# Prompt attention with its query tiles taken in turns from both ends, two banks for the transposed probabilities, and a bank for each output tile

## The chip, the cores and the metric

The kernel runs on one core of one Trainium2 chip. The metric is the device time of one execution in microseconds (us). The engines are named as in the profile: PE is TensorE (PEld its weight loads), DVE is VectorE, ACT is ScalarE, POOL is GpSimd, SP is SyncE, which here issues most DMAs. PSUM, the memory that PE writes its results to, has eight banks of 2 KB in each of its 128 partitions.

## The reference

One decoder layer for a prompt of 1024 tokens and for eight samples of four tokens. The change lies in the prompt's attention. Its core is this: for every head, the query at position i meets the keys at or before it, gets a bias by distance, and a softmax:

```
logits = einsum(q, k) * ATT_SCALE + bias          # bias by T5 bucket of i - j
probs  = softmax(where(mask, logits, -1e30))
out    = einsum(probs, v)
o_b    = gates[0] * o_cmp + gates[1] * o_slc + gates[2] * o_win
```

Three kinds of it are computed in the stage: mixer A (eight heads; the three dilated windows are merged into one table of biases and masks), the selected branch of mixer B and its window branch of 512 tokens (eight query heads each, in two groups that share keys and values). The gates are sigmoids of projected values. All query tiles are independent of each other, so they may be computed in any order.

## The kernel before

`prompt_attention` handles three kinds times four pairs of heads, twelve iterations (`it`), of eight units each (`u`, 96 in all). A unit is one tile of 128 queries (`qt`, 0 to 7) for the two heads of a pair. It meets `nk` key tiles of 128 keys: `qt + 1` of them, and in the last kind at most five. `parts(u)` gives these numbers. In this kernel `qt` is `u % 8`, so within an iteration the units grow from one key tile to eight (36 tiles in all, 30 in an iteration of the last kind), and then the next iteration starts with one again.

The order of work is written out by hand, engine by engine, in steps `s`. In step `s`

- PE computes the scores of unit s into `psS` (two chunks of 512 keys are held, L672), then the transposes of the probabilities of unit s-2 into banks of `psT` (four 128x128 blocks to a bank, L690), then the products with the values of unit s-3 into `psO` (L711) and, in the same tile of `psO`, a transpose of the softmax weights (L717);
- DVE adds the bias and takes the maximum of unit s (`logits`, L821, then L827 and L831, which writes the negated maximum `nm`), copies those banks of unit s-2 from `psT` to `PT` that are its own (`copies`, L847), takes a reciprocal for unit s-1 (L835) and multiplies out unit s-3 (`finish`, L859);
- ACT copies the other banks of unit s-2 (L789), then computes the exponentials of unit s (L795) and copies the weight row `Rs` of unit s-3 (L802);
- POOL widens the reciprocals (L753, L758), adds up the branches in `mixT` (L769), and reverses the queries of the next iteration (L738).

The banks of transposed probabilities are numbered through the stage. DVE copies every bank whose number leaves 2 when divided by 3 (`on_dve`), ACT the others. `psT` has three banks, so PE may write bank b once bank b-3 was copied. Both tiles of `psO` lie in one bank, and the value products of unit u wait until `finish` of unit u-1 is done (semaphore `s_wt`). With `psS` at four banks, all eight banks are in use.

The gates are brought into reversed order by one product (L705) into `psO` ahead of the values of unit 8; ACT turns them into sigmoids (L776) at the start of step 11, and PE waits for that. SP loads queries, keys, biases and values of iteration it+1 once all units of iteration it-1 are finished (`load`).

Of the kernel before, what the change touches and what calls it, by code (L numbers as in the profile page):

```python
# [9 lines left out]
ACT = mybir.ActivationFunctionType  # L10
AXX = mybir.AxisListType.X

P = 128
# [520 lines left out]

def prompt_attention(nc, io, scr, mixT, wo, cv, s_mix, s_wo, s_cvl):
    QT = SEQ // P
    NKIND = 3
    NIT = NKIND * 4
    U = NIT * QT

    kinds = [
        dict(tab="tabA", tab0=7172 - A0, q0=0, k0=0, v="new_a_v_p", gate=None, back=QT),
        dict(tab="tabS", tab0=7172, q0=8, k0=8, v="new_slc_v_p", gate=1, back=QT),
        dict(tab="tabW", tab0=7172 - W0, q0=8, k0=10, v="vw", gate=2, back=LW // P),
    ]

    def parts(u):

        it, qt = u // QT, u % QT
        j0 = max(0, qt - kinds[it // 4]["back"])  # L550
        return it, it // 4, it % 4, qt, j0, qt + 1 - j0

    chunk0, bank0 = [0], [0]
    for u in range(U):
        nk = parts(u)[5]
        chunk0.append(chunk0[-1] + -(-nk // 4))
        bank0.append(bank0[-1] + -(-2 * nk // 4))

    def on_dve(bank):
        return bank % 3 == 2  # L560

    def copied(bank):

        return bank - bank // 3, bank // 3

    with ExitStack() as stack:
        m = Mem(nc, stack, "pa")
        gates = m.sb("gates", [P, QT, 24])
        gsig = m.sb("gsig", [P, QT, 24])
        ident = m.sb("ident", [P, P])  # L570
        flip = m.sb("flip", [P, P])
# [6 lines left out]
        PT = m.sb("PT", [P, 3, 2 * SEQ])  # L578
# [6 lines left out]
        tmp = m.sb("tmp", [P, 4, P])  # L585
        Rs = m.sb("Rs", [P, 4, P])
        psS = m.ps("psS", [P, 2, 2, 512])
        psT = m.ps("psT", [P, 3, 512])
        psO = m.ps("psO", [P, 2, 2 * P])
        s_id = m.sem("identity_loaded")  # L590
        s_gl = m.sem("gates_loaded")
        s_mc = m.sem("compressed_rows_loaded")
        s_gf = m.sem("gates_flipped")
        s_gs = m.sem("gates_ready")
# [8 lines left out]
        s_ca = m.sem("probs_t_copied_by_act")  # L603
        s_cd = m.sem("probs_t_copied_by_dve")
# [4 lines left out]
        s_wt = m.sem("weighted")  # L609
# [50 lines left out]
        @block.tensor  # L660
        def _(pe):
            def scores(u):
                it, ki, p, qt, j0, nk = parts(u)
                i = it % 2
                for c in range(chunk0[u], chunk0[u + 1]):
                    k0 = (c - chunk0[u]) * 512
                    w = min(512, nk * P - k0)
                    if c >= 2:
                        pe.wait_ge(s_lg, 2 * (c - 1))
                    for h in range(2):  # L670
                        r = slice(h * HD, h * HD + HD)
                        pe.matmul(psS[:, c % 2, h, 0:w], qT[r, i, qt * P:qt * P + P],  # L672
                                  kT[r, i, j0 * P + k0:j0 * P + k0 + w], start=True, stop=True).then_inc(s_qk, 1)

            def transposes(u):
                nk = parts(u)[5]
                if u == 0:
                    pe.wait_ge(s_id, 16)
                pe.wait_ge(s_ex, 2 * (u + 1))
                for b in range(bank0[u], bank0[u + 1]):  # L680
                    if b >= 3:
                        na, nd = copied(b - 2)
                        if on_dve(b - 3):
                            pe.wait_ge(s_cd, nd)
                        else:
                            pe.wait_ge(s_ca, na)
                    x0 = 4 * (b - bank0[u])
                    for x in range(x0, min(x0 + 4, 2 * nk)):
                        j, h = x // 2, x % 2
                        mm = pe.transpose(psT[:, b % 3, (x - x0) * P:(x - x0) * P + P],  # L690
                                          L[:, u % 3, h, j * P:j * P + P], ident[:, :])
                    mm.then_inc(s_tr, 1)

            def values(u):
                it, ki, p, qt, j0, nk = parts(u)
                i = it % 2
                na, nd = copied(bank0[u + 1])
                pe.wait_ge(s_ca, na)
                if nd:
                    pe.wait_ge(s_cd, nd)  # L700
                if u:
                    pe.wait_ge(s_wt, u)
                if u == QT:
                    pe.wait_ge(s_gl, 32)
                    pe.matmul(psO[:, u % 2, 0:QT * 24], flip[:, :],  # L705
                              gates[:, :, :].rearrange("p t n -> p (t n)"), start=True, stop=True).then_inc(s_gf, 1)
                    pe.wait_ge(s_gs, 1)
                for j in range(nk):
                    for h in range(2):
                        v0 = h * HD if ki == 0 else 0  # L710
                        mm = pe.matmul(psO[h * HD:h * HD + HD, u % 2, 0:P], V[:, i, j0 + j, v0:v0 + HD],  # L711
                                       PT[:, u % 3, (2 * j + h) * P:(2 * j + h) * P + P],
                                       start=(j == 0), stop=(j == nk - 1))
                        if j == nk - 1:
                            mm.then_inc(s_pv, 1)
                pe.wait_ge(s_rg, u + 1)
                pe.transpose(psO[:, u % 2, P:2 * P], rgB[:, u % 4, :, :].rearrange("p h d -> p (h d)"),  # L717
                             ident[:, :]).then_inc(s_pv, 1)

            for s in range(U + 3):  # L720
                if s < U:
                    if s % QT == 0:
                        it = s // QT
                        pe.wait_ge(s_ld[it % 2], 96 * (it // 2 + 1))
                        pe.wait_ge(s_qr, it + 1)
                    scores(s)
                if 2 <= s < U + 2:
                    transposes(s - 2)
                if s >= 3:
                    values(s - 3)  # L730
# [40 lines left out]
        @block.scalar  # L771
        def _(act):
            for s in range(U + 3):
                if s == QT + 3:
                    act.wait_ge(s_gf, 1)
                    nc.scalar.activation(gsig[:, :, :], psO[:, QT % 2, 0:QT * 24].rearrange("p (t n) -> p t n", t=QT),  # L776
                                         ACT.Sigmoid).then_inc(s_gs, 1)
                if 2 <= s < U + 2:
                    u = s - 2
                    nk = parts(u)[5]  # L780
                    if u >= 3:
                        act.wait_ge(s_pv, 3 * (u - 2))
                    for b in range(bank0[u], bank0[u + 1]):
                        if on_dve(b):
                            continue
                        x0 = 4 * (b - bank0[u]) * P
                        w = min(512, 2 * nk * P - x0)
                        act.wait_ge(s_tr, b + 1)
                        nc.scalar.activation(PT[:, u % 3, x0:x0 + w], psT[:, b % 3, 0:w], ACT.Copy).then_inc(s_ca, 1)  # L789
                if s < U:  # L790
                    w = parts(s)[5] * P
                    act.wait_ge(s_nm, s + 1)
                    for h in range(2):
                        x = L[:, s % 3, h, 0:w]
                        nc.scalar.activation(x, x, ACT.Exp, bias=nm[:, s, h:h + 1], scale=1.0,  # L795
                                             accum_out=sm[:, s, h:h + 1]).then_inc(s_ex, 1)
                if s >= 3:
                    u = s - 3
                    act.wait_ge(s_pv, 3 * (u + 1))
                    if u >= 4:  # L800
                        act.wait_ge(s_wt, u - 3)
                    nc.scalar.activation(Rs[:, u % 4, :], psO[:, u % 2, P:2 * P], ACT.Copy).then_inc(s_rs, 1)  # L802

        @block.vector
        def _(dve):
# [31 lines left out]
            def copies(u):  # L837
                nk = parts(u)[5]
                for b in range(bank0[u], bank0[u + 1]):
                    if not on_dve(b):  # L840
                        continue
                    x0 = 4 * (b - bank0[u]) * P
                    w = min(512, 2 * nk * P - x0)
                    if u >= 3:
                        dve.wait_ge(s_pv, 3 * (u - 2))
                    dve.wait_ge(s_tr, b + 1)
                    dve.tensor_copy(PT[:, u % 3, x0:x0 + w], psT[:, b % 3, 0:w]).then_inc(s_cd, 1)  # L847

            def finish(u):
                it, ki, p, qt, j0, nk = parts(u)  # L850
# [2318 lines left out]
```

## Time and profile before

| | |
|---|---|
| median of 3 runs | 2502.0 us (2500.79 to 2505.6) |
| profiled execution | 2500.79 us |
| its span in the trace | 2499.0 us |
| prompt attention in the trace | about 1068 to 1482 us |
| PE, DVE, ACT, POOL busy, share of the whole span | 91%, 39%, 23%, 19% |
| PE, DVE, ACT busy, 1068 to 1482 us | 354, 237, 241 us of 414 |

The shares are averages over stages with different limits. In the stage that is changed, PE shows busy for 85% of the time, but with matmuls that overlap and whose ends are modelled, and with gaps at semaphores in every step; DVE and ACT are each busy for somewhat less than 60%. What sets its length is to be read from the waits and from the order of events in single steps.

### The profile page before, as it was taken

The numbers are of one execution on the slowest core, as the hardware profiler recorded it, in microseconds if no ns is written. First come the engines' busy times: TensorE is split into PE (matmuls) and PEld (weight loads), VectorE is DVE, ScalarE is ACT, GpSimd is POOL, SyncE is SP. The second block draws the span as 40 slices with busy tenths as digits, with TensorE's granted clock in tenths as the row PEclk, the third lists the DMA queues.
The fourth block names the chain that finished last, engine by engine and source line by source line (L and its number), as shares of the span: only waits on it lengthen the run. The fifth ranks groups of instructions, "written<-read, shape, count | busy, mean of one in ns | idle before, by whom it ended". The sixth has DMA issues, their size and how long they took to land. (4 is left out here: it accounts for less than half of the span.)

```text
span 2499.0 us, 34990 instructions
## 1 busy us (share of the span) xinstructions
PE 2268.6 (91%) x13904; PEld 1475.1 (59%) x13904; DVE 977.2 (39%) x2333; ACT 572.6 (23%) x1255; POOL 466.1 (19%) x664
## 2 busy tenths in 40 slices
PE   7999997999488687678888889999999999999998
PEld 3445666666254555445555654488888888744443
DVE  3001002333133354355555642277677675500210
ACT  3000002333022133255555641111101111100110
POOL 1314211221100344200121220022233222100000
PEclk8999997999788899899999999999999999999999
DMA  6712114776476777641222422165656542500110
GB/s 230 230 69 79 46 41 183 284 285 242 154 262 246 273 297 308 248 140 61 60 77 77 128 66 78 59 219 185 224 182 236 190 149 68 205 32 0 61 37 17
DMA packets 162360, 376.33 MB, mean 151 GB/s; under 512 B 44231, under 2 KB 100911, under 8 KB 144272
## 3 DMA queue, kind: packets, MB, share of 16 engines
q1 hardware_dynamic: 128284, 148.68, 18.9%
q0 software_dynamic: 25216, 149.43, 15.6%
q10 hardware_dynamic: 8698, 75.99, 8.8%
q8 instruction: 111, 1.82, 0.3%
q14 instruction: 51, 0.41, 0.1%
HBM read 345.71 MB, written 99.65 MB: 178 GB/s over the span
## 5 line engine op out<-in xcount | busy, mean ns | idle before, releaser
L2674 PE MATMUL ff_ps<-ff_hx,ff_aw 128*128 128x264 f32 x2464 | 550.1, 386 | 0.9 <-DVE ff_hx L2913 0.9
L2674 PEld LDWEIGHTS ff_ps<-ff_hx,ff_aw 128*128 128x128 f32 x2464 | 467.3, 190 | 80.8 <-issue 1.2
L369 PE MATMUL in_ps<-in_w,in_xT 128*128 128x512 f32 (+1 forms) x512 | 199.6, 545 | 0.0
L795 ACT ACTIVATE pa_L<-pa_L,pa_nm 128x640 f32<-128x640 f32 (+3 forms) x192 | 142.0, 741 | 143.7 <-DVE pa_nm L831 143.5
L369 PEld LDWEIGHTS in_ps<-in_w,in_xT 128*128 128x128 f32 x512 | 95.2, 190 | 93.6 <-issue 84.9
L821 DVE CUSTOM_DVE_ANT_0 pa_L<-pa_psS,pa_T 128x512 f32<-128x512 f32 (+3 forms) x288 | 138.4, 530 | 29.1 <-PE pa_psS L672 28.1
L491 DVE TENSOR_SCALAR in_yout<-in_ps 128x512 f32<-128x512 f32 (+2 forms) x44 | 26.1, 593 | 300.3 <-PE in_ps L369 190.9
L711 PE MATMUL pa_psO<-pa_PT,pa_V 128*64 128x128 f32 x1632 | 112.6, 282 | 33.6 <-DVE pa_tmp L859 21.9
L690 PE MATMUL pa_psT<-pa_ident,pa_L 128*128 128x128 f32 x816 | 115.1, 281 | 22.2 <-DVE pa_PT L847 14.1
L672 PE MATMUL pa_psS<-pa_kT,pa_qT 64*128 64x512 f32 (+3 forms) x576 | 115.3, 506 | 21.2 <-POOL pa_qT L738 18.4
L1064 DVE COPY cmp_KT<-cmp_psT 128x512 f32<-128x512 f32 x128 | 88.6, 692 | 97.6 <-PE cmp_psT L980 96.8
L690 PEld LDWEIGHTS pa_psT<-pa_ident,pa_L 128*128 128x128 f32 x816 | 87.2, 141 | 64.7 <-issue 29.5
L711 PEld LDWEIGHTS pa_psO<-pa_PT,pa_V 128*64 128x64 f32 x1632 | 90.7, 139 | 52.2 <-issue 47.9
L383 PE MATMUL in_ps<-in_xT,in_w 128*128 128x352 f32 x384 | 113.9, 459 | 0.0
L990 PE MATMUL cmp_psH<-cmp_KT,pre_w 64*64 64x512 f32 x1024 | 113.3, 592 | 0.0
L2633 PE MATMUL ff_ps<-ffn_G 128*128 128x512 f32 x256 | 111.9, 596 | 0.0
L2856 ACT ACTIVATE ff_work<-ff_work 128x1056 f32<-128x1056 f32 x22 | 23.8, 1083 | 369.8 <-DVE ff_work L3008 369.8
L3035 DVE TENSOR_TENSOR ff_work<-ff_ps,ff_work 128x512 f32<-128x512 f32 (+1 forms) x18 | 12.3, 685 | 238.0 <-PE ff_ps L2752 139.3
L1077 ACT ACTIVATE cmp_KT<-cmp_psT 128x512 f32<-128x512 f32 x128 | 76.5, 598 | 104.4 <-PE cmp_psT L980 104.3
L2099 PE MATMUL sb_psT<-sb_ident,sel_space 128*128 128x128 f32 x512 | 72.2, 290 | 28.8 <-ACT sel_space L2245 15.0
L2702 PE MATMUL ff_ps<-ff_hx,ffn_G 128*128 128x512 f32 x224 | 97.4, 592 | 0.0
L383 PEld LDWEIGHTS in_ps<-in_xT,in_w 128*128 128x128 f32 x384 | 72.8, 190 | 40.5 <-issue 0.2
(381 smaller groups left out, 3042.2 us busy)
## 6 DMA issues: line engine op xcount, KB each, us to landing
out_new_a_k_s<-in_cache_a_k ACTq DMA_DIRECT2D x8, 4088.0 KB
out_new_a_v_s<-in_cache_a_v ACTq DMA_DIRECT2D x8, 4088.0 KB
ff_aw<-in_w_up SPq DMA_DIRECT2D x44, 512.0 KB, 7.1
in_w<-in_w_in SPq DMA_DIRECT2D x5, 2048.0 KB, 19.0
sel_space<-in_cache_a_k SPq DMA_DIRECT2D x8, 1024.0 KB
sel_space<-in_cache_a_v SPq DMA_DIRECT2D x8, 1024.0 KB
ff_hx<-in_w_down SPq DMA_DIRECT2D x14, 512.0 KB, 4.3
sel_space<-in_cache_a_k SPq DMA_DIRECT2D x24, 256.0 KB
```

The costliest lines, as they stand in the source:

```text
L369: mm = pe.matmul(ps[0:n, b, 0:width], xT[:, k, t * P:t * P + n], w[:, ch % WBUF, k, 0:width], start=(k == 0), stop=(k == KC - 1))
L383: mm = pe.matmul(ps[:, b, 0:n], w[:, ch % WBUF, k, c * P:c * P + P], xT[:, k, r0:r0 + n], start=(k == 0), stop=(k == KC - 1))
L672: pe.matmul(psS[:, c % 2, h, 0:w], qT[r, i, qt * P:qt * P + P], kT[r, i, j0 * P + k0:j0 * P + k0 + w], start=True, stop=True).then_inc(s_q ...
L690: mm = pe.transpose(psT[:, b % 3, (x - x0) * P:(x - x0) * P + P], L[:, u % 3, h, j * P:j * P + P], ident[:, :])
L711: mm = pe.matmul(psO[h * HD:h * HD + HD, u % 2, 0:P], V[:, i, j0 + j, v0:v0 + HD], PT[:, u % 3, (2 * j + h) * P:(2 * j + h) * P + P], star ...
L795: nc.scalar.activation(x, x, ACT.Exp, bias=nm[:, s, h:h + 1], scale=1.0, accum_out=sm[:, s, h:h + 1]).then_inc(s_ex, 1)
L821: dve.tensor_tensor_reduce(L[:, u % 3, h, 512 * x:512 * x + n], psS[:, c % 2, h, 0:n], T[:, it % 2, h, SEQ - w + 512 * x:SEQ - w + 512 * x ...
L990: mm = pe.matmul(psH[odd_t * HD:odd_t * HD + HD, p % 2, h, 0:w], pre.w1[r, kv, t + odd_t, :], x(r, odd_t), start=first, stop=last, tile_po ...
L1064: copy(KT[:, n % 2, 4 * x:4 * x + 4, j * P:j * P + P], psT[:, u % 3, :].rearrange("p (t n) -> p t n", t=4)).then_inc((s_ca, s_cd)[which], 1)
L2633: mm = pe.matmul(ps[:, j % 6, :], mixT[:, k, t * P:t * P + P], wo[:, k, half * 512:half * 512 + 512], start=(k == 0), stop=(k == KC - 1))
L2674: mm = pe.matmul(ps[:, bank_of(x, j, g), 0:H2], aw[:, j % 2, at, k, :], hx[:, bt, k, g * H2:g * H2 + H2], start=(k == 0), stop=(k == KH - 1))
L2702: mm = pe.matmul(ps[:, bank[i] + half, :], G[:, k, t * P:t * P + P], wd(k)[:, half * 512:half * 512 + 512], start=(k == 0), stop=(k == NFF ...
```

## The change

Four edits, all in `prompt_attention`:

1. `parts(u)` takes its query tile from `TURNS = [0, 7, 1, 6, 2, 5, 3, 4]`. The units of an iteration then have 1, 8, 2, 7, 3, 6, 4, 5 key tiles (in the last kind 1, 5, 2, 5, 3, 5, 4, 5).
2. `psT` has two banks instead of three: PE may write bank b once bank b-2 was copied. Which banks DVE copies goes on by the same rule (number modulo 3).
3. `psO` is two whole banks, one for each tile; the values of unit u wait for `finish` of unit u-2.
4. The sigmoid of the gates is moved from the start of step 11 on ACT to its end, just ahead of the weight row of unit 8; the product that feeds it goes to the upper half of the bank, and PE waits for it only before the values of unit 10.

```
+    TURNS = [0, 7, 1, 6, 2, 5, 3, 4]
...
-        it, qt = u // QT, u % QT
+        it, qt = u // QT, TURNS[u % QT]
...
-        psT = m.ps("psT", [P, 3, 512])
-        psO = m.ps("psO", [P, 2, 2 * P])
+        psT = m.ps("psT", [P, 2, 512])
+        psO = m.ps("psO", [P, 2, 512])
...
-                    if b >= 3:
-                        na, nd = copied(b - 2)
-                        if on_dve(b - 3):
+                    if b >= 2:
+                        na, nd = copied(b - 1)
+                        if on_dve(b - 2):
                             pe.wait_ge(s_cd, nd)
                         else:
                             pe.wait_ge(s_ca, na)
...
-                if u:
-                    pe.wait_ge(s_wt, u)
+                if u >= 2:
+                    pe.wait_ge(s_wt, u - 1)
                 if u == QT:
                     pe.wait_ge(s_gl, 32)
-                    pe.matmul(psO[:, u % 2, 0:QT * 24], flip[:, :],
+                    pe.matmul(psO[:, u % 2, 2 * P:2 * P + QT * 24], flip[:, :],
                               gates[:, :, :].rearrange("p t n -> p (t n)"), start=True, stop=True).then_inc(s_gf, 1)
+                if u == QT + 2:
                     pe.wait_ge(s_gs, 1)
...
-                if s == QT + 3:
-                    act.wait_ge(s_gf, 1)
-                    nc.scalar.activation(gsig[:, :, :], psO[:, QT % 2, 0:QT * 24].rearrange("p (t n) -> p t n", t=QT),
-                                         ACT.Sigmoid).then_inc(s_gs, 1)
...
                     if u >= 4:
                         act.wait_ge(s_wt, u - 3)
+                    if u == QT:
+                        act.wait_ge(s_gf, 1)
+                        nc.scalar.activation(gsig[:, :, :], psO[:, u % 2, 2 * P:2 * P + QT * 24].rearrange("p (t n) -> p t n", t=QT),
+                                             ACT.Sigmoid).then_inc(s_gs, 1)
```

How the order moves (`pa_psS` is psS of this stage, and so on; sizes are those of one result): on PE, the first iteration, from the scores of unit 3 on. Before (scores of four key tiles, transposes of two, values of one; then five, three, two):

```order
L672 MATMUL pa_psS<-pa_kT,pa_qT 128x512 x2
L690 MATMUL pa_psT<-pa_ident,pa_L 128x128 x4
L711 MATMUL pa_psO<-pa_PT,pa_V 64x128 x2
L717 MATMUL pa_psO<-pa_ident,pa_rgB 128x128
L672 MATMUL pa_psS<-pa_kT,pa_qT 128x512 x2
L672 MATMUL pa_psS<-pa_kT,pa_qT 128x128 x2
L690 MATMUL pa_psT<-pa_ident,pa_L 128x128 x6
L711 MATMUL pa_psO<-pa_PT,pa_V 64x128 x4
L717 MATMUL pa_psO<-pa_ident,pa_rgB 128x128
```

And now, on PE at the same place (scores of seven key tiles, transposes of eight, values of one; then three, two, eight):

```order
L673 MATMUL pa_psS<-pa_kT,pa_qT 128x512 x2
L673 MATMUL pa_psS<-pa_kT,pa_qT 128x384 x2
L691 MATMUL pa_psT<-pa_ident,pa_L 128x128 x16
L713 MATMUL pa_psO<-pa_PT,pa_V 64x128 x2
L719 MATMUL pa_psO<-pa_ident,pa_rgB 128x128
L673 MATMUL pa_psS<-pa_kT,pa_qT 128x384 x2
L691 MATMUL pa_psT<-pa_ident,pa_L 128x128 x4
L713 MATMUL pa_psO<-pa_PT,pa_V 64x128 x16
L719 MATMUL pa_psO<-pa_ident,pa_rgB 128x128
```

Large scores now stand beside large transposes and small values, and small scores beside small transposes and large values. The sixteen transposes fill four banks of a `psT` that holds two.

On ACT, the same iteration, before, steps 4 to 6 (exponentials of five, six and seven key tiles):

```order
L789 ACTIVATE pa_PT<-pa_psT 128x256
L795 ACTIVATE pa_L,pa_sm<-pa_L,pa_nm 128x640 x2
L802 ACTIVATE pa_Rs<-pa_psO 128x128
L789 ACTIVATE pa_PT<-pa_psT 128x512
L795 ACTIVATE pa_L,pa_sm<-pa_L,pa_nm 128x768 x2
L802 ACTIVATE pa_Rs<-pa_psO 128x128
L789 ACTIVATE pa_PT<-pa_psT 128x512 x2
L795 ACTIVATE pa_L,pa_sm<-pa_L,pa_nm 128x896 x2
```

And now on ACT, steps 3 to 5 (exponentials of seven, three and six key tiles):

```order
L787 ACTIVATE pa_PT<-pa_psT 128x512 x3
L793 ACTIVATE pa_L,pa_sm<-pa_L,pa_nm 128x896 x2
L804 ACTIVATE pa_Rs<-pa_psO 128x128
L793 ACTIVATE pa_L,pa_sm<-pa_L,pa_nm 128x384 x2
L804 ACTIVATE pa_Rs<-pa_psO 128x128
L787 ACTIVATE pa_PT<-pa_psT 128x512 x2
L787 ACTIVATE pa_PT<-pa_psT 128x256
L793 ACTIVATE pa_L,pa_sm<-pa_L,pa_nm 128x768 x2
```

All of ACT's copies of a unit still stand ahead of the exponentials of the same step. On DVE the order within a step is the same as before; this is step 3 now, logits of seven key tiles, then the one bank of the unit of eight that is DVE's:

```order
L823 ISA pa_L,pa_mx<-pa_psS,pa_T 128x384
L823 ISA pa_mx 128x1
L829 TENSOR_TENSOR pa_mm<-pa_mx 128x2
L833 TENSOR_SCALAR pa_nm<-pa_mm 128x2
L849 COPY pa_PT<-pa_psT 128x512
L837 RECIPROCAL pa_rg<-pa_sm 128x2
L861 TENSOR_TENSOR ffn_G<-pa_psO,pa_Rs 128x128
```

DVE's copy comes behind the logits of a unit of seven key tiles, where before it came behind those of a unit two tiles larger than the one copied.

## Rows read from the trace of the kernel before

**Rows 1.** Waits, 1068 to 1482 us: engine, releaser; total us, times, longest us.
```profile
ACT pa_L L795 <- DVE pa_nm L831: 143.5, 76, 23.0
...
DVE pa_tmp L859 <- ACT pa_Rs L802: 99.0, 64, 3.0
...
PE pa_psO L711 <- DVE pa_tmp L859: 21.9, 35, 0.9
```

**Rows 2.** Timeline, a six-tile step: start, length, engine, line, instruction [idle before].
```profile
1262.92 0.29 DVE L859 TENSOR_TENSOR pa_tmp<-pa_psO,pa_Rs 128x128 f32<-128x128 f32 x1 [1.90 <-ACT pa_Rs L802]
1263.13 0.68 DVE L821 CUSTOM_DVE_ANT_0 pa_L<-pa_psS,pa_T 128x512 f32<-128x512 f32 x1
...
1265.35 0.17 DVE L831 TENSOR_SCALAR pa_nm<-pa_mm 128x2 f32<-128x2 f32 x1
1265.42 0.69 DVE L847 COPY pa_PT<-pa_psT 128x512 f32<-128x512 f32 x1
1265.55 0.94 ACT L795 ACTIVATE pa_L<-pa_L,pa_nm 128x768 f32<-128x768 f32 x1 [2.08 <-DVE pa_nm L831]
...
1267.69 0.29 DVE L859 TENSOR_TENSOR pa_tmp<-pa_psO,pa_Rs 128x128 f32<-128x128 f32 x1 [1.50 <-ACT pa_Rs L802]
```

**Rows 3.** Timeline, other starts of the finishing instruction L859.
```profile
1258.63 0.29 DVE L859 TENSOR_TENSOR pa_tmp<-pa_psO,pa_Rs 128x128 f32<-128x128 f32 x1 [1.14 <-ACT pa_Rs L802]
...
1272.94 0.29 DVE L859 TENSOR_TENSOR pa_tmp<-pa_psO,pa_Rs 128x128 f32<-128x128 f32 x1 [1.72 <-ACT pa_Rs L802]
...
1278.67 0.29 DVE L859 TENSOR_TENSOR pa_tmp<-pa_psO,pa_Rs 128x128 f32<-128x128 f32 x1 [1.93 <-ACT pa_Rs L802]
...
1281.69 0.29 DVE L859 TENSOR_TENSOR pa_tmp<-pa_psO,pa_Rs 128x128 f32<-128x128 f32 x1 [1.43 <-ACT pa_Rs L802]
...
1423.46 0.29 DVE L859 TENSOR_TENSOR pa_tmp<-pa_psO,pa_Rs 128x128 f32<-128x128 f32 x1 [1.47 <-ACT pa_Rs L802]
...
1426.98 0.29 DVE L859 TENSOR_TENSOR pa_tmp<-pa_psO,pa_Rs 128x128 f32<-128x128 f32 x1 [1.14 <-ACT pa_Rs L802]
```

**Rows 4.** Timeline, the first L859 and that of unit 92.
```profile
1077.03 0.29 DVE L859 TENSOR_TENSOR ffn_G<-pa_psO,pa_Rs 128x128 f32<-128x128 f32 x1 [1.68 <-ACT pa_Rs L802]
...
1474.28 0.29 DVE L859 TENSOR_TENSOR pa_tmp<-pa_psO,pa_Rs 128x128 f32<-128x128 f32 x1 [1.29 <-ACT pa_Rs L802]
```

**Rows 5.** Timeline, copies, transposes and value products where large follows small.
```profile
1275.98 0.69 DVE L847 COPY pa_PT<-pa_psT 128x512 f32<-128x512 f32 x1
...
1276.73 1.09 PE L690 MATMUL pa_psT<-pa_ident,pa_L 128*128 128x128 f32 x8 [0.77 <-DVE pa_PT L847]
...
1278.55 1.49 ACT L789 ACTIVATE pa_PT<-pa_psT 128x512 f32<-128x512 f32 x3
...
1279.55 1.53 PE L711 MATMUL pa_psO<-pa_PT,pa_V 128*64 128x128 f32 x24
...
1281.90 1.53 PE L690 MATMUL pa_psT<-pa_ident,pa_L 128*128 128x128 f32 x12
...
1283.09 1.08 ACT L789 ACTIVATE pa_PT<-pa_psT 128x512 f32<-128x512 f32 x2 [1.44 <-PE pa_psT L690]
```

**Rows 6.** Timeline, ScalarE around the sigmoid.
```profile
1108.15 1.28 ACT L776 ACT_TABLE_LOAD   x1
...
1109.68 0.33 ACT L776 ACTIVATE pa_gsig<-pa_psO 128x192 f32<-128x192 f32 x1 [0.25 <-PE pa_psO L705]
```

**Rows 7.** Stretches: length; busy PE, PEld, DVE, ACT, POOL; PEclk, DMA share, GB/s.
```profile
1070.00:1072.00 2.00, 2.00 (x7) 0.68 (x6) 1.43 (x10) 1.43 (x7) 0.29 (x1) 0.50 1.04 375
...
1241.00:1243.00 2.00, 0.59 (x6) 0.43 (x8) 1.37 (x8) 1.66 (x6) 0.00 (x0) 1.00 0.00 0
1243.00:1247.00 4.00, 4.00 (x32) 2.93 (x29) 0.79 (x4) 0.28 (x1) 0.81 (x2) 0.57 0.02 4
...
1265.00:1267.00 2.00, 2.00 (x15) 1.20 (x12) 1.12 (x6) 1.45 (x3) 0.73 (x2) 1.00 0.03 5
```

**Rows 8.** Timeline, the first load of a later iteration on SyncE's queue.
```profile
1254.82 0.32 SPq L623 DMA_DIRECT2D pa_qL<-scr_qT  x1
```

More of the change, by code:

```diff
@@ L689, in transposes @@
                         j, h = x // 2, x % 2
-                        mm = pe.transpose(psT[:, b % 3, (x - x0) * P:(x - x0) * P + P],
+                        mm = pe.transpose(psT[:, b % 2, (x - x0) * P:(x - x0) * P + P],
                                           L[:, u % 3, h, j * P:j * P + P], ident[:, :])
@@ L788, in _ @@
                         act.wait_ge(s_tr, b + 1)
-                        nc.scalar.activation(PT[:, u % 3, x0:x0 + w], psT[:, b % 3, 0:w], ACT.Copy).then_inc(s_ca, 1)
+                        nc.scalar.activation(PT[:, u % 3, x0:x0 + w], psT[:, b % 2, 0:w], ACT.Copy).then_inc(s_ca, 1)
                 if s < U:
@@ L846, in copies @@
                     dve.wait_ge(s_tr, b + 1)
-                    dve.tensor_copy(PT[:, u % 3, x0:x0 + w], psT[:, b % 3, 0:w]).then_inc(s_cd, 1)
+                    dve.tensor_copy(PT[:, u % 3, x0:x0 + w], psT[:, b % 2, 0:w]).then_inc(s_cd, 1)
             def finish(u):
```

## The prediction

> **What bounds the kernel now.** I read the waits of the attention stage first, then the timeline of single steps. The two longest waits of working engines point at each other: ACT waits for DVE's negated maximum before the exponentials (143.5 us over 76 times), and DVE waits for ACT's weight row before it finishes a unit (99.0 us in the two kinds of mixer B alone) [rows 1]. The wait that the change takes away, value products behind the finish of the unit before, shows 21.9 us in the same two kinds.
>
> The timeline of a step of six key tiles shows why the first two are a loop [rows 2]: finish at 1262.92, logits from 1263.13, maximum at 1265.35, exponentials from 1265.55, and the next finish at 1267.69, as soon as ACT has copied the weight row behind them. No PE instruction is in it. Finish to exponentials is 2.63 us (DVE's half), exponentials to finish 2.14 us (ACT's half), together 4.77. The order in which DVE and ACT do this doesn't change: the exponentials of step s stand between the logits of s and the finish at the end of s.
>
> The length of this loop follows from the number of key tiles of unit s. Five tiles take 1262.92 - 1258.63 = 4.29 us, eight 1278.67 - 1272.94 = 5.73 [rows 2, 3]: 0.48 per tile. Four tiles, with one chunk less, take 1426.98 - 1423.46 = 3.52, so that I take 3.04, 2.56 and 2.08 for three, two and one. That is 31.24 us for an iteration of 1 to 8 and 28.36 for one of the last kind. All twelve: 8 x 31.24 + 4 x 28.36 = 363.4 us.
>
> What the stage takes beyond it is the only thing that a better order can give back. From the first finish (end of step 3) to that of unit 92 (end of step 95) it is 1474.28 - 1077.03 = 397.25 us [rows 4]. The loop accounts for 363.4 less 11.2 of steps 0 to 3, so 352.2. 45.0 us are left, nearly all in the three or four steps after the turn from large to small. There the loop is short and PE has the largest transposes and value products to do: the step of one tile takes 1281.69 - 1278.67 = 3.02 us in place of 2.08 [rows 3], since the value products begin only at 1279.55 [rows 5].
>
> **The change, part by part.** *The turns.* Each step keeps its loop length, so 363.4 stays. PE's work is levelled. Transposes cost 0.22 us a tile (1.53 us for twelve, which is six tiles, 1.09 for eight), and value products the same (1.53 for six tiles) [rows 5], and scores about the same by their number of columns. With 0.56 for the gaps between the parts, as I read them at those starts, an iteration costs PE about 36 x 3 x 0.22 + 8 x 0.56 = 28.3 us against 31.24 of the loop. Following the starts through one iteration, PE is ready in every step but one: in the step of the large unit after the smallest, its scores come 0.05 to 0.4 us late in the first two kinds, and 0.7 in the last, where that step's loop is short. I take 8 x 0.3 + 3 x 0.7 = 4.5 us. So all of the 45.0 goes and 4.5 comes back. If PE keeps up everywhere this is 0; if PE set the time of the four small steps, as 3.02 against 2.08 did, it is 48 x 0.94 = 45.
>
> *A bank of its own for each output tile.* The wait of 21.9 us goes. Only where PE was late did it reach the loop, and that is in the 45.0 already. Nothing is added.
>
> *Two banks for the transposes.* This takes something away that the trace of before can't show. Within a step ACT's copies of unit s-2 stand ahead of its exponentials, and DVE's copy of unit s-2 stands behind its logits (the copy starts at 1265.42, after the maximum at 1265.35 [rows 2]). With three banks, bank b waits for bank b-3, and if DVE copies b-3 it copies b too: ACT never waits for a bank behind DVE's copy of the same unit. With two, the bank two behind one of DVE's is ACT's, and it can't be transposed before DVE is through with the logits. ACT then holds the exponentials behind this chain: logits, DVE copy, transposes, ACT copy. From the moment at which the exponentials could have started the price is: copy starts 0.13 earlier [rows 2], takes 0.69, PE starts 0.06 after its end (1276.73 against 1275.98 + 0.69), four transposes 0.66 (eight take 1.09, at 0.11 apiece), about 0.1 to ACT (at 1283.09 it starts behind eight transposes that began at 1281.90), and 0.5 until ACT goes on after a copy (three take 1.49, of which each occupies about 0.45 to 0.6) [rows 5]. The sum is 1.87. Where the late bank holds two blocks it is 0.22 less for PE and 0.2 less for the shorter copy: 1.45.
>
> It happens in units of three or four banks in which DVE has the first bank, or the second of four. Counting banks modulo 3 (20 in an iteration, 18 in the last kind), two of the large units of each iteration have it: in the first two kinds 11 times with a full bank and 5 times with a half one, in the last kind 8 times with a half one. So 11 x 1.87 + 13 x 1.45 = 39.4 us. All these lie in steps with large logits, and the loop has no slack there. Bounds: if ACT's other copies or late scores had delayed the step anyway, down to 24 x 0.8 = 19; if each also held up PE's values of the next step, 24 x 2.3 = 55. I take 39.4, since each piece has a row.
>
> *The sigmoid.* Before, a table load of 1.28 us, the sigmoid (0.33) [rows 6] and a second such load ahead of the exponentials stood in step 11, with DVE's logits beside them; what they cost is in the 45.0. Now the first load and the sigmoid come behind the exponentials of step 11, on the path: 1.6. The second comes ahead of step 12's exponentials, beside short logits: 0.4. I take 2.0, between 1.2 and 3.
>
> *The start.* PE begins at the lower clock (0.50 from 1070 to 1072 [rows 7]), and now with scores of eight tiles instead of two: 0.8.
>
> *Loads.* An iteration's loads start in the third step of the one before (1254.82 [rows 8]) and are through by about 1265 [rows 7]. POOL wants them in its seventh step, about 15 us behind the start now against 18 before. Covered by some 4 us.
>
> *The clock.* In a held-up step PE does nothing from its second bank to the end of the logits, up to 3.1 us. Between 1243 and 1247 the granted clock was 0.57 of full, of its levels of 2.4 and 1.2 GHz mostly the lower, and in the two microseconds before it fell PE was busy for 0.59 [rows 7]. At the lower one, value products in the next step come up to 1.7 late against a slack of 1.2. I take 0.5 us in 9 of the 24 steps, 4.5; 0 and 24 x 0.94 = 22.6 are the ends.
>
> *Sum.* 4.5 + 39.4 + 2.0 + 0.8 + 4.5 = 51.2 come and 45.0 go: 6.2 us more. On the profiled execution (2500.8, which is also the fastest of the three) that is 2507; on the median of 2502.0 it is 2508.
>
> **The rivals.**
>
> *The clock decides (slower by more).* Each held-up step is followed by a stretch at half clock. Then four transposes inside the chain take 0.44 more and the next step 0.5. 22.6 in place of 4.5 gives 24 us more, 2526. For it: idle stretches of up to 3.1 us now come twice an iteration, longer than the 1.4 us in the row before the fall. Against it: PE stood still at each turn of iteration before, and the stage's clock shows only this fall and one like it. The Trainium skill ("TensorE: Matmul & The Clock Gate", "Why this matters for your kernels") says in its table that idle gaps between bursts of matmuls put the engine back to its lower clock; by that rule most held-up steps would lose it, and this rival would hold.
>
> *The levelling wins (faster).* The hand-over costs less than the sum of its pieces, because in steps with large logits the first scores are late or DVE's maximum comes before the copies that ACT has to do anyway; it decides below 1.4 us a time, where 24 hand-overs cost less than what the levelling gives after its other costs (33 us). At its lower bound of 19 us the sum is 14 less: 2488. For it: 45 us are really there to be had, and PE has slack. Against it: in the rows of step 6 nothing overlaps the wait of 2.08 us before the exponentials.
>
> *Nothing changes.* Late scores and clock cost nothing: 2502.0 - 45.0 + 42.2 = 2499, within what can be told apart.
>
> **How the numbers follow.** A change of less than 0.2%, 5 us, can't be told from none here. The forecast's case (sum between 0 and +12) has 0.47, the clock 0.16, the levelling 0.20, no change 0.17. The forecast's case falls on both sides of +5: about 0.29 slower and 0.18 same. So slower is 0.45, same 0.35, faster 0.20. The range, 2492 to 2521, leaves out the outer halves of the two rivals; the likeliest case alone is 2502 to 2514.
>
> **What would show it.** In the profile of after: waits of PE's value products for L861 gone; the step of one key tile near 2.1 us between finishes, and the wait of ACT's weight row for PE near nothing. The held-up steps: two in each iteration, in the first iteration step 3, with an exponential start about 1.9 us after the maximum and PE's transposes waiting for DVE's copy. Their count of 24 and the sum of about 39 us is the core. I am wrong if ACT starts exponentials straight after the maximum there, if the small steps remain at 3 us, or if the stage's length, 414 us before, is not about 420.

## The result and the profile after

The changed kernel takes 2530.7 us (median of 4 runs, 2525.2 to 2534.9) against 2503.0 of the kernel before in the same comparison: a ratio of 1.0099 (95% interval 1.0073 to 1.0127), or 25 us more in 2500 by the fast runs. I had forecast 2508, in a range from 2492 to 2521: slower was right, the size was not. The profiled execution took 2522.6 us; another 19 of the same kernel lie between 2518 and 2539.

The stage from the first finish to that of unit 92, first after as a stretch (columns as in rows 7), then the same two instructions as in [rows 4]:

```profile
1076.63:1495.10 418.47, 364.87 (x3000) 243.92 (x2999) 225.33 (x949) 236.62 (x611) 69.03 (x162) 0.92 0.23 67
```

```profile
1076.63 0.29 DVE L861 TENSOR_TENSOR ffn_G<-pa_psO,pa_Rs 128x128 f32<-128x128 f32 x1 [3.51 <-ACT pa_Rs L804]
...
1495.10 0.29 DVE L861 TENSOR_TENSOR pa_tmp<-pa_psO,pa_Rs 128x128 f32<-128x128 f32 x1 [2.66 <-ACT pa_Rs L804]
```

418.47 us against 397.25. The loop of logits, exponentials and finish accounts for 347.8 of it (363.4 less the four first steps, which now have 1, 8, 2 and 7 key tiles), so 70.7 us are beyond the loop, where 45.0 were before. The forecast for this stretch is 48.5: the 51.2 of the sum also hold the first of the 24 hand-overs (1.87, in step 3) and the start (0.8), and both lie ahead of the first finish. The stretch's PEclk, the granted clock of PE as a share of full speed, is 0.92. Counted in stretches of 1 us, about 64 us are at the lower clock, where before there were 7 (PEclk 0.99).

The waits of the stage after (engine, releaser; total, times, longest):

```profile
ACT pa_PT L787 <- PE pa_psT L691: 142.5, 110, 3.5
DVE pa_tmp L861 <- ACT pa_Rs L804: 113.2, 64, 3.5
...
PE pa_psT L691 <- DVE pa_PT L849: 46.0, 24, 3.5
ACT pa_L L793 <- DVE pa_nm L833: 41.7, 47, 3.4
```

ACT waited 143.5 us for DVE's maximum before the exponentials [rows 1]; now that is 41.7, and 142.5 go to PE's transposes: ACT has to copy them before it comes to the exponentials. PE's wait for DVE's copy appears 24 times: the 24 hand-overs that the bank numbers gave (a hand-over is the chain of the prediction, DVE's copy, then PE's transposes, then ACT's copy, ahead of the exponentials). PE's wait for the finish, 21.9 us in [rows 1], is gone.

One hand-over, in the step of seven key tiles of iteration 3 (counted from 0):

```profile
1181.55 0.29 DVE L861 TENSOR_TENSOR ffn_G<-pa_psO,pa_Rs 128x128 f32<-128x128 f32 x1 [1.26 <-ACT pa_Rs L804]
...
1184.25 0.17 DVE L833 TENSOR_SCALAR pa_nm<-pa_mm 128x2 f32<-128x2 f32 x1
1184.33 0.69 DVE L849 COPY pa_PT<-pa_psT 128x512 f32<-128x512 f32 x1
...
1185.07 0.66 PE L691 MATMUL pa_psT<-pa_ident,pa_L 128*128 128x128 f32 x4 [1.61 <-DVE pa_PT L849]
...
1185.77 0.60 ACT L787 ACTIVATE pa_PT<-pa_psT 128x512 f32<-128x512 f32 x1 [1.67 <-PE pa_psT L691]
1186.26 1.03 ACT L793 ACTIVATE pa_L<-pa_L,pa_nm 128x896 f32<-128x896 f32 x1
...
1188.61 0.29 DVE L861 TENSOR_TENSOR ffn_G<-pa_psO,pa_Rs 128x128 f32<-128x128 f32 x1 [3.52 <-ACT pa_Rs L804]
```

Maximum at 1184.25; without the hand-over the exponentials would start 0.20 later, at 1184.45, as in [rows 2]. They start at 1186.26: 1.81 us late, where I had 1.87. The step takes 7.06 for a loop of 5.25. DVE's copy, PE's transposes and ACT's copy follow one another as written down.

Most short steps did what was forecast as well. From 1170.50 to 1172.62 is the step of one key tile, 2.12 us where [rows 3] had 3.02:

```profile
1170.50 0.29 DVE L861 TENSOR_TENSOR ffn_G<-pa_psO,pa_Rs 128x128 f32<-128x128 f32 x1 [1.45 <-ACT pa_Rs L804]
...
1172.62 0.29 DVE L861 TENSOR_TENSOR ffn_G<-pa_psO,pa_Rs 128x128 f32<-128x128 f32 x1 [0.54 <-ACT pa_Rs L804]
```

Three of the four steps of one key tile in the last kind did not: they take 3.69 us.

What was not forecast in its size is this. Two stretches around a hand-over of the next iteration, and the timeline behind them:

```profile
1210.00:1214.00 4.00, 2.12 (x25) 1.42 (x23) 2.20 (x8) 1.87 (x3) 0.40 (x1) 1.00 0.00 0
1214.00:1218.00 4.00, 4.00 (x29) 2.73 (x29) 1.55 (x8) 2.62 (x9) 0.40 (x1) 0.57 0.00 0
```

```profile
1215.60 2.19 PE L713 MATMUL pa_psO<-pa_PT,pa_V 128*64 128x128 f32 x20
...
1217.71 0.33 PE L719 MATMUL pa_psO<-pa_ident,pa_rgB 128*128 128x128 f32 x1
...
1217.97 1.77 PE L673 MATMUL pa_psS<-pa_kT,pa_qT 64*128 64x512 f32 x8
1218.08 0.28 ACT L804 ACTIVATE pa_Rs<-pa_psO 128x128 f32<-128x128 f32 x1
...
1218.39 0.29 DVE L861 TENSOR_TENSOR ffn_G<-pa_psO,pa_Rs 128x128 f32<-128x128 f32 x1 [1.25 <-ACT pa_Rs L804]
...
1219.28 0.69 DVE L823 CUSTOM_DVE_ANT_0 pa_L<-pa_psS,pa_T 128x512 f32<-128x512 f32 x1 [0.59 <-PE pa_psS L673]
...
1220.43 1.09 ACT L787 ACTIVATE pa_PT<-pa_psT 128x512 f32<-128x512 f32 x2 [2.07 <-PE pa_psT L691]
...
1222.26 0.60 ACT L787 ACTIVATE pa_PT<-pa_psT 128x512 f32<-128x512 f32 x1 [0.75 <-PE pa_psT L691]
...
1222.76 1.03 ACT L793 ACTIVATE pa_L<-pa_L,pa_nm 128x896 f32<-128x896 f32 x1
...
1225.11 0.29 DVE L861 TENSOR_TENSOR pa_tmp<-pa_psO,pa_Rs 128x128 f32<-128x128 f32 x1 [2.49 <-ACT pa_Rs L804]
```

PE was busy for 2.12 of 4 us, and the clock fell (0.57 in the next four). The value products, 1.31 us for twenty at full clock, take 2.19, so that the weight row and, behind it, the scores of the next unit leave PE late: the scores start at 1217.97, 0.42 us ahead of the finish. This step itself, one of two key tiles, takes 2.83 us, only 0.27 more than without a fall. The larger price is paid in the step behind it, one of seven key tiles without a hand-over: DVE waits 0.59 for the scores, ACT copies the first two banks at 1220.43, the last bank of the eight-tile unit only at 1222.26, and the exponentials start at 1222.76. 6.72 us for 5.25.

In the kernel of the first experiment below, in which the clock doesn't fall, the same two steps are these:

```profile
1192.51 1.77 PE L673 MATMUL pa_psS<-pa_kT,pa_qT 64*128 64x512 f32 x8
...
1194.22 0.29 DVE L866 TENSOR_TENSOR ffn_G<-pa_psO,pa_Rs 128x128 f32<-128x128 f32 x1 [0.97 <-ACT pa_Rs L809]
...
1197.29 1.03 ACT L798 ACTIVATE pa_L<-pa_L,pa_nm 128x896 f32<-128x896 f32 x1
...
1199.64 0.29 DVE L866 TENSOR_TENSOR pa_tmp<-pa_psO,pa_Rs 128x128 f32<-128x128 f32 x1 [1.88 <-ACT pa_Rs L809]
```

The scores start 1.71 us ahead of the finish, the exponentials 3.07 behind it (4.37 with the fall), and the step takes 5.42: the fall costs the large step 1.30 us.

The trace has 18 falls of the clock, and each begins in one of the 24 held-up steps. The Trainium skill ("TensorE: Matmul & The Clock Gate", "Why this matters for your kernels") says that idle gaps between matmuls bring the lower clock back. The trace agrees: the longest idle gap of PE in the row of 2.12 us is 1.89, its wait for DVE's copy.

### The profile page after: what moved, and what is told of

It reads as the page before. It is cut to its first block and busy times, and to the rows that moved or that the text cites. A ratio compares the mean times of both kernels' runs of the same rounds, so it can differ in the third digit from the quotient of the medians.

```text
span 2520.8 us, 34991 instructions
## 1 busy us (share of the span) xinstructions
PE 2296.2 (91%) x13904; PEld 1488.2 (59%) x13904; DVE 964.5 (38%) x2333; ACT 578.9 (23%) x1255; POOL 468.2 (19%) x664
## 3 DMA queue, kind: packets, MB, share of 16 engines
q1 hardware_dynamic: 128284, 148.68, 18.7%
## 5 line engine op out<-in xcount | busy, mean ns | idle before, releaser
L691 PE MATMUL pa_psT<-pa_ident,pa_L 128*128 128x128 f32 x816 | 132.7, 300 | 56.1 <-DVE pa_PT L849 46.0
L691 PEld LDWEIGHTS pa_psT<-pa_ident,pa_L 128*128 128x128 f32 x816 | 93.9, 149 | 110.7 <-DVE pa_PT L849 51.7
L793 ACT ACTIVATE pa_L<-pa_L,pa_nm 128x128 f32<-128x128 f32 (+3 forms) x192 | 142.0, 742 | 64.5 <-DVE pa_nm L833 64.3
L673 PE MATMUL pa_psS<-pa_kT,pa_qT 64*128 64x512 f32 (+3 forms) x576 | 123.2, 536 | 18.2 <-POOL pa_qT L740 18.0
L713 PE MATMUL pa_psO<-pa_PT,pa_V 128*64 128x128 f32 x1632 | 122.3, 298 | 0.0
L787 ACT ACTIVATE pa_PT<-pa_psT 128x512 f32<-128x512 f32 (+1 forms) x155 | 81.1, 540 | 143.1 <-PE pa_psT L691 142.5
L713 PEld LDWEIGHTS pa_psO<-pa_PT,pa_V 128*64 128x64 f32 x1632 | 97.7, 149 | 19.2 <-issue 18.3
L383 PEld LDWEIGHTS in_ps<-in_xT,in_w 128*128 128x128 f32 x384 | 72.8, 190 | 40.5 <-issue 0.2
```

The source lines that it names most:

```text
L383: mm = pe.matmul(ps[:, b, 0:n], w[:, ch % WBUF, k, c * P:c * P + P], xT[:, k, r0:r0 + n], start=(k == 0), stop=(k == KC - 1))
L691: mm = pe.transpose(psT[:, b % 2, (x - x0) * P:(x - x0) * P + P], L[:, u % 3, h, j * P:j * P + P], ident[:, :])
```

## The experiments

These ran on three chips, on which the kernel before takes 2478 to 2481 us; times are compared as ratios, and the expectations' absolute times, written with 2503 in mind, are to be read as differences from it. Spans of the stage are set side by side all the same: in the three profiled kernels that keep the old order and the loop, on two of these chips and in the profile of before, undisturbed steps of five to eight key tiles agree within 0.02 us. "Beyond the loop" is the span from first finish to that of unit 92, less the loop's share (352.2 us in the old order, 347.8 with the turns). The turns have 4.4 us less of the loop in that span and as much more ahead of it.

| kernel | ratio to before (95%) | first finish to unit 92 | beyond the loop | PEclk |
|---|---|---|---|---|
| before | 1 | 397.25 | 45.0 | 0.99 |
| changed | 1.0099 (1.0073 to 1.0127) | 418.47 | 70.7 | 0.92 |
| changed, again | 1.0122 (1.0095 to 1.0149) | 412.67 | 64.9 | 0.94 |
| filler, 16 transposes | 1.0014 (1.0001 to 1.0026) | 393.97 | 46.2 | 1.00 |
| filler, 8 transposes | 1.0025 (1.0011 to 1.0040) | 397.30 | 49.5 | 0.99 |
| DVE's last banks | 0.9823 (0.9803 to 0.9842) | 353.08 | 5.3 | 1.00 |
| the same, shared psO | 0.9948 (0.9928 to 0.9967) | 378.02 | 30.2 | 1.00 |
| the same, old order | 1.0063 (1.0038 to 1.0088) | 409.09 | 56.9 | 0.97 |
| turns only | 0.9963 (0.9950 to 0.9977) | 384.26 | 36.5 | 0.98 |
| two banks only | 1.0125 (1.0100 to 1.0150) | 426.70 | 74.5 | 0.96 |
| last banks, early row | 0.9804 (0.9770 to 0.9838) | 351.28 | 3.5 | 1.00 |
| before, early row | 0.9748 (0.9717 to 0.9779) | 339.45 | -12.7 | 1.00 |

"Changed, again" and both fillers were profiled on other chips than "changed"; the first of them and "filler, 8" ran on the same one.

My theory after the result: the loop and the 24 hand-overs are as forecast, and what was missed is the price of the clock. The rivals: the turns themselves cost, or hand-overs are dearer than their pieces.

**Filler against the clock.**

```
+                    if b - bank0[u] >= 2 and on_dve(b - 2):
+                        if u >= 2:
+                            pe.wait_ge(s_wt, u - 2)
+                        for x in range(16):
+                            pe.transpose(psO[:, (u - 1) % 2, 384:512], ident[:, :], ident[:, :])
```

> The changed kernel, where PE, before it waits for DVE's copy inside a unit, makes 16 transposes of the identity into an unused part of psO (1.75 us of work that nobody reads). Theory that the falls of the clock cost some 20 us beyond the hand-overs: the falls become few (under six in the stage), the hand-overs stay, the time goes to about 2507, between 2500 and 2514. Rival (the falls are a mark of idle time and cost next to nothing, what was missed is a dearer hand-over): 2525 to 2535, unchanged.

Measured: 1.0014. The stage, and the filler's own instructions:

```profile
1058.09:1452.06 393.97, 375.21 (x3360) 264.84 (x3358) 223.53 (x948) 234.63 (x612) 69.08 (x162) 1.00 0.24 71
```

```profile
L686 PE MATMUL pa_psO<-pa_ident x384: 272/273/273, 1052.9 to 1448.0; 128*128 128x128 f32 x192
```

384 transposes are 16 in each of 24 places: the count of hand-overs, by the program's own rule. The clock is at full all through. 46.2 us beyond the loop are left; the forecast for the stretch without its clock term is 48.5 - 4.5 = 44.0. More work for PE made the kernel 1% faster, so the falls were a cause.

With eight transposes in place of 16:

> The changed kernel with 8 transposes of filler in each of the 24 held-up steps instead of 16, so that PE's idle stretch there shrinks by 0.9 us only. If the falls follow from the idle stretch, fewer than the changed kernel's 18 and more than none; between the two in time, 5 to 20 us above the kernel before. If any work inside the wait does it, as with 16: no fall and the kernel before plus 3.

Measured: 1.0025, PEclk 0.99, and the changed kernel again, on the same chip, 1.0122 at 0.94. With 0.9 us of filler three falls are left. The intervals of 8 and 16 overlap, so whether 8 is a little worse in time stays open; its 49.5 us lie between. The four profiles stand in one order: 64 us at the lower clock and 70.7 beyond the loop, 53 and 64.9, 10 and 49.5, none and 46.2.

```profile
1058.62:1455.92 397.30, 360.65 (x3176) 248.03 (x3174) 223.69 (x948) 234.49 (x612) 69.07 (x162) 0.99 0.24 70
```

```profile
1058.66:1471.33 412.67, 358.28 (x2984) 239.42 (x2981) 224.95 (x948) 235.73 (x611) 69.05 (x162) 0.94 0.23 68
```

> The changed kernel again, on the chip of this call, so that the others stand beside it. By the result 1.0% above the kernel before, by 0.7 to 1.3%; with some 18 falls of the clock in the stage and about 70 us beyond the loop.

The time held. The falls and the 70 us did not: 14 falls in the stretch, again all in held-up steps, and 64.9 us. The number of falls differs from execution to execution.

**The hand-overs taken away.** DVE copies only the last bank of a unit of three or four:

```
-        return bank % 3 == 2
+        return bank in dve_banks     # last bank of each unit with 3 or 4
```

> The changed kernel with another choice of DVE's banks: DVE copies the last bank of each unit of three or four banks and no other. No bank of ACT's then stands behind DVE's copy of its unit. Theory: the 24 held-up steps go, PE is idle for less, the clock stays up; 7 us beyond the loop are left where the kernel before has 45: 2465, between 2458 and 2478, with fewer than six falls of the clock in the stage. Rival (PE's lateness in large steps comes from the turns or the two banks as such): 2500 or above.

Measured: 0.9823, 44 us below the kernel before, with all four edits in place.

```profile
1053.87:1406.95 353.08, 336.83 (x3014) 225.68 (x3012) 201.38 (x920) 250.48 (x640) 68.80 (x162) 1.00 0.27 79
```

5.3 us beyond the loop, where the terms for late PE and the sigmoid are 6.5 (the start lies ahead of the stretch), and no fall of the clock. The difference to filler, 46.2 - 5.3 = 40.9, is the measured price of the 23 hand-overs in the stretch; by the prediction they are 10 x 1.87 + 13 x 1.45 = 37.5. 37.1 of the 40.9 are in the held-up steps themselves: 1.80 us for a full bank and 1.4 for a half one in most, 1.4 in steps of eight key tiles with either. The rest is mostly in large steps without a hand-over. In two of the held-up steps the filler itself costs 0.55, which makes 1.1 of the 40.9.

From the first logits of the stage to its last finish it is 371.4 us, against 411.9 in the profile of before: 40.5 less. The other 4 us lie outside the stage, which this profiled execution reaches 2 to 4 us sooner than the three others of that chip (turns only, two banks only, filler 16), without an edit there.

**Two banks alone, in the old order.**

```
-        psT = m.ps("psT", [P, 3, 512])
+        psT = m.ps("psT", [P, 2, 512])      # and the waits for b-2
```

> The kernel before with psT at two banks and nothing else. Theory: in the old order too a bank of ACT's stands two behind one of DVE's in units of three or four banks, two units an iteration on average in the first two kinds and none in the last; in steps of large logits 1.45 to 1.87 us each, at the turn of iteration about 1. Some 20 us above the kernel before, 2515 to 2530. Rival (two banks are as good as three): 2503.

Measured: 1.0125, 31 us above. The large steps with a hand-over have 1.6 us (seven tiles) and 2.7 to 3.4 us (eight) more than the loop, and the two smallest steps 19 us each in seven iterations, where before they had 12 and 15. So two banks with this rule cost in the old order too; it is above my 20 and above the 12 to 27 of the expectation. PEclk is 0.96, and how much of the 31 is the clock's isn't separated.

**The turns alone**, with the sigmoid behind ACT's copies of step 11.

> The kernel before with the turns alone: three banks of psT and one shared bank of psO stay, the sigmoid moves behind ACT's copies of step 11 (with the turns PE would otherwise wait for ever). Theory (two banks of psT behind DVE's copy, and the falls of the clock that the idle PE then has, make the loss; the turns by themselves gain): no hand-over DVE copy, transposes, ACT copy inside a step, few falls of the clock. The 45 us beyond the loop go, about 24 come back from value products that wait for the finish before them: 2482, between 2470 and 2495. Rival (the turns themselves cost, since large transposes now stand beside large scores and PE is late): at or above the changed kernel, 2520 to 2535.

Measured: 0.9963, 9 us below; the theory had 20 (with a range from 8 to 33), the rival a loss. The turns don't cost. That they gain less than I thought I put down to the shared bank of psO: value products wait for the finish (24.9 + 13.9 us of PE, against 21.9 in [rows 1] and 9.3 in the first kind before), and large steps behind are late, those of six and seven key tiles by 0.8 us in most. Step 11, with the sigmoid in its new place, takes 9.09 for 5.25:

```profile
PE pa_psO L712 <- DVE pa_tmp L860: 24.9, 29, 1.8
...
PE pa_psO L712 <- DVE ffn_G L860: 13.9, 14, 1.8
```

**What each buffer and the order are worth.** Both with DVE's last banks and two banks of psT. First psO shared as before:

> Turns, two banks of psT and DVE copying only last banks, but both tiles of psO in one bank as before, with the wait for the finish of the unit before (and the sigmoid behind the copies of step 11). It prices the second bank of psO. By the loop: value products start 0.44 us behind each finish, so that small steps and the scores of the next large step come 0.5 to 0.8 late, some 20 us in all: 25 us beyond the loop, about 20 us below the kernel before. Rival (the second bank of psO is worth nothing, since the wait taken away was off the path): as with two banks of psO, 44 us below.

Measured: 0.9948, 13 us below the kernel before, where I had 20; 30.2 us beyond the loop for 25 forecast. Against DVE's last banks that is 24.9 more. 2.2 of it are in step 11, where this kernel has the sigmoid ahead of the exponentials (9.15 us against 6.90); so the bank for each output tile is worth about 23 us of the stage once the turns are there. I had given it nothing.

Then the old order of the query tiles, everything else as in the fast version:

> Two banks of psT, DVE copying only last banks, a bank for each tile of psO, but the query tiles in their old order. It prices the turns. PE then has 3.8 and 4.3 us of work in the two steps whose loop is 2.1 and 2.6, after a lead of about 2 us: about 30 us beyond the loop, 15 us below the kernel before. Rival (the turns are worth nothing once PE no longer waits): 44 us below as well; the other way, if two banks hurt at the turn of iteration, level with the kernel before.

Measured: 1.0063, slower than before, a miss for all three numbers. At the turn of iteration the step of one key tile takes mostly 2.9 us beyond its loop (with the unit of seven in transposes and that of six in value products), that of two 2.5. I take it that two banks hold PE there, since ACT copies the banks of a large unit one by one behind its weight row; that isn't shown by itself. Seen from the fast version the turns are worth 52 us of the stage, with a part for the clock that isn't separated (PEclk 0.97 against 1.00). So neither the turns nor the banks give the gain alone.

**The loop itself.** All sums rest on the claim that logits, exponentials, weight row and finish are one loop. If so, copying the weight row ahead of the exponentials must open it.

```
 (ACT, in each step)
+                if s >= 3:  # wait for PE, copy Rs of unit s-3
                 if s < U:   # exponentials of unit s
-                if s >= 3:  # wait for PE, copy Rs of unit s-3
```

> The kernel before with that one edit: the weight row copied ahead of the exponentials. If the loop sets the large steps, they become shorter (eight key tiles from 5.7 to about 4.5 us), while the small steps at the turn, where PE is late, stay or grow, since its lead is smaller: PE needs the same 28 us an iteration plus its waits for one shared bank of psO, some 31 to 34: 15 to 35 us below the kernel before. Rival (PE's wait for the finish closes a loop of its own at the same length): within 5 us of it.

Measured: 0.9748, 62 us below the kernel before, with this edit alone; the lowest ratio of all. The large steps are shorter than the loop by 0.8 (eight tiles) to 2.0 us (some of five). A step of five key tiles:

```profile
1300.71 0.28 ACT L795 ACTIVATE pa_Rs<-pa_psO 128x128 f32<-128x128 f32 x1
...
1300.94 0.17 DVE L831 TENSOR_SCALAR pa_nm<-pa_mm 128x2 f32<-128x2 f32 x1
...
1301.09 0.27 DVE L859 TENSOR_TENSOR pa_tmp<-pa_psO,pa_Rs 128x128 f32<-128x128 f32 x1
...
1301.14 0.83 ACT L801 ACTIVATE pa_L<-pa_L,pa_nm 128x640 f32<-128x640 f32 x1 [0.15 <-DVE pa_nm L831]
1301.88 1.09 PE L690 MATMUL pa_psT<-pa_ident,pa_L 128*128 128x128 f32 x8
...
1304.08 0.28 ACT L795 ACTIVATE pa_Rs<-pa_psO 128x128 f32<-128x128 f32 x1 [0.41 <-PE pa_psO L717]
...
1304.63 0.27 DVE L859 TENSOR_TENSOR pa_tmp<-pa_psO,pa_Rs 128x128 f32<-128x128 f32 x1
```

The finish at 1301.09 stands ahead of the exponentials at 1301.14 and no longer waits for them; 3.54 us to the next one, where [rows 2, 3] had 4.29. The clock is at 1.00 too. I had 15 to 35 us, so this is a miss; what bounds the steps now I haven't shown.

> The kernel with turns, two banks of psT, DVE copying last banks and a bank for each tile of psO, in which ACT also copies the weight row of unit s-3 (and makes the sigmoid) ahead of the exponentials of unit s instead of behind them. If the stage's length is set by the loop logits, exponentials, weight row, finish, this cuts the loop: DVE's finish no longer waits for the exponentials of the same step, DVE and ACT work side by side, and PE's own work (28.3 us an iteration in the first two kinds, about 25 in the last) is the next bound: 326 to 345 us for the steps in place of 369, 25 to 40 us below the kernel with DVE's last banks, so 2.6 to 3.4% below the kernel before. Rival (something else is the bound, such as PE already now): within 5 us of the kernel with last banks, 1.8% below.

Measured: 0.9804, which can't be told from 0.9823. The theory's 2.6 to 3.4% failed and the rival's number (within 5 us of DVE's last banks) held, but not its reading that nothing changes: the loop opens (the eight-tile steps take 0.75 less than it), but the steps of one and three tiles take 1.1 and 0.55 more, because ACT now waits for PE's value products before its exponentials:

```profile
ACT pa_Rs L799 <- PE pa_psO L721: 68.0, 83, 1.3
```

With the turns a small step has the largest value products, and ACT stands behind them. Why the old order with three banks does better by 0.6% than this one I haven't shown.

## Why the prediction was wrong

- *The loop and the 45.0 us beyond it*: right. In the profiles that keep the old order and the loop, steps of five to eight key tiles have its length within 0.02 us (but for one late step of five, and the six with a hand-over in "two banks only"), and opening the loop made the steps shorter.
- *The turns give the 45.0 back*: right as a mechanism. With the hand-overs gone the small steps take 2.1, 2.5, 3.0 and 3.5 us and 5.3 us are left in all. It needs the own bank of psO, though, to which I gave no value of its own: with the turns it is worth about 23 us.
- *The hand-overs*: right in count (24) and nearly in size, 40.9 us for the 23 in the stretch against 37.5.
- *Late PE, sigmoid*, 6.5: 5.3 measured. *Start*, 0.8: the first four steps with DVE's last banks take 1.0 us more over their loop than before.
- *The clock, 4.5*: the step that failed, by its size; the mechanism was there. I took 0.5 us in 9 of the 24 held-up steps. The trace has falls in 18 of them, 14 in the second profile, and changed less filler is 70.7 - 46.2 = 24.5 us, and 18.7 with the second: about 1.4 us a fall. Both factors were off. I also looked for the price in the wrong place. Of the 24.5 us, 2.5 are in held-up steps, 11.3 in the small steps directly behind them and 9.9 in the large steps two behind. The slack of 1.2 us that I set against a fall did not cover it: three steps of one key tile in the last kind take 3.69 us, where with the filler they take 2.12, and large steps without a hand-over take up to 1.3 us more, as in the rows above.

My rival "the clock decides", with a drop behind each hand-over, gave 2526 and had a chance of 0.16. Its kind was right and its 22.6 us are about what was measured, but in part by luck: it has 24 falls at 0.94 us (0.44 inside the chain, 0.5 behind it), where the trace has fewer and dearer ones, with 2.5 us in all in the held-up steps.

With 24.5 for 4.5 the sum is +26 us, against +25 measured. That it fits so well is luck too. The stage itself, from its first logits to the finish of unit 92, grew by 28.3 us, which is, within 0.1, the sum of 24.5 for the clock, 42.6 for the 24 hand-overs (1.7 for the first) and 6.3 for the rest, less 45.0. The profiled execution of before reaches the stage 7.5 us later than that of after, without an edit ahead of it.

## What to carry to other kernels

A ring of buffers and a rule that shares its slots between two engines belong together: count, for each slot, whose copy frees it and what stands ahead of that copy in its engine's program. Price an idle stretch of PE by what the lower clock does to the steps behind it, and not to the one in which it idles. And where two engines alternate and neither is busy for much over half the time, look first for the one instruction that closes their loop: moving it was worth more here (62 us) than all buffers and the turns together (44).

## What the runs showed of the hardware

Sixteen transposes whose results nobody reads, in the gaps of 24 steps, made the program 0.8 to 1.1% faster (1.0014 against 1.0099 and 1.0122). And the clock fell behind stretches in which PE still was busy half of the time: 2.12 of 4 us in the row above, at full clock. It was no different before: [rows 7] show the 2 us ahead of the fall with 0.59 busy, and the 4 us ahead of it have this:

```profile
1239.00:1243.00 4.00, 2.08 (x18) 1.67 (x20) 1.53 (x8) 3.66 (x11) 0.81 (x2) 1.00 0.00 0
```
